# Prompt attention: the value matmuls of a pair of heads alternate on the column halves of the array

## The reference, cut to what matters

```python
def block(i):                      # 128 queries, keys 0 .. 128*(i+1)-1 matter
    s = (einsum('bqhn,bkhn->bhqk', qn, k_nope) + einsum('bqhr,bkr->bhqk', qr, k_rope)) * scale
    s = where(key_pos[None, :] <= q_pos[:, None], s, -inf)
    p = softmax(s, axis=-1)
    return einsum('bhqk,bkhv->bqhv', p, v)
out = lax.map(block, arange(T // 128))
```

## Time and profile before

| what | value |
|---|---|
| median of three runs | 2098.39 us |
| the profiled execution | 2094.72 us |
| its span (first to last instruction) | 2092.9 us |
| PE busy | 1940.1 us, 93% of the span |
| DVE busy, ACT busy | 1298.1 us, 507.9 us |
| prompt attention | from about 508 us to 702 us of the span |
| values L877 | 79.6 us busy, 576 records |
| scores L857 | 76.5 us busy, 192 records |
| turns L690 of `Pr` | 47.5 us busy, 288 records |
| copies of turned probabilities, ACT L1304 | 32.9 us busy, 64 |

### The profile page before, as it was taken

How to read it: one execution, slowest core, us unless ns; L and a number is a source line. 1 busy time by engine, 2 the same in 40 slices (tenths; PEclk the granted TensorE clock), 3 DMA queues, 4 the chain that set the end, 5 groups by cost and what they waited for, 6 DMA issues and landing times.

```text
span 2092.9 us, 34720 instructions
## 1 busy us (share of the span) xinstructions
PE 1940.1 (93%) x15054; PEld 1669.1 (80%) x15054; DVE 1298.1 (62%) x1566; ACT 507.9 (24%) x865; POOL 512.5 (24%) x383
## 2 busy tenths in 40 slices
PE   6989989978999799996989779999999999999988
PEld 5978878876576544446988649999999999999987
DVE  5565665585666688874342545787288277385664
ACT  5222221134543255552120323110011000010013
POOL 2211111221000133431224103232332323323321
PEclk8999999998999899996999989999999999999998
DMA  4101202111000489871122412111211211211112
GB/s 142 41 21 52 52 21 52 39 34 40 1 1 1 181 327 351 327 269 41 51 61 61 154 58 61 41 41 39 63 41 36 60 47 31 61 41 51 46 28 92
DMA packets 157268, 165.12 MB, mean 79 GB/s; under 512 B 18486, under 2 KB 143436, under 8 KB 152988
## 3 DMA queue, kind: packets, MB, share of 16 engines
q1 hardware_dynamic: 142538, 82.70, 13.6%
q0 software_dynamic: 7168, 75.50, 9.5%
q10 hardware_dynamic: 7412, 4.71, 0.7%
HBM read 153.95 MB, written 9.03 MB: 78 GB/s over the span
## 4 chain that ended last, share of the span: by engine, by line
PE 73%; DVE 19%; ACT 4%; issue 2%; DMA 1%; SPq 0%; ACTq 0%; POOL 0%; DVEq 0%
PE PS L671 16%; PE PS L672 15%; PE PS L673 15%; PE PS L690 4%; PE PS L924 4%; PE PS L877 4%; DVE cu L1992 3%; PE PS L954 3%; PE PS L857 3%; PE PS L734 2%; DVE ct L1978 2%; PE PS L914 1%; PE PS L939 1%; DVE Sst L1609 1%; DVE atail L1982 1%
## 5 line engine op out<-in xcount | busy, mean ns | idle before, releaser
L621 POOL CAST whi<-wraw 128x1024 fp32r<-128x1024 f32 (+4 forms) x146 | 131.1, 898 | 1189.7 <-PE PS L673 1064.9
L671 PE MATMUL PS<-BH,whi 128*128 128x344 f32 x1152 | 370.3, 321 | 3.5 <-ACT RB L1136 3.5
L672 PE MATMUL PS<-BL,whi 128*128 128x344 f32 x1152 | 369.2, 320 | 0.0
L673 PE MATMUL PS<-BH,wlo 128*128 128x344 f32 x1152 | 368.9, 320 | 0.0
L623 POOL TENSOR_TENSOR wlo<-wraw,whi 128x1024 fp32r<-128x1024 f32 (+4 forms) x146 | 292.9, 2006 | 11.7
L671 PEld LDWEIGHTS PS<-BH,whi 128*128 128x128 f32 x1152 | 218.1, 189 | 4.0 <-ACT RB L1136 4.0
L672 PEld LDWEIGHTS PS<-BL,whi 128*128 128x128 f32 x1152 | 218.0, 189 | 0.0
L673 PEld LDWEIGHTS PS<-BH,wlo 128*128 128x128 f32 x1152 | 218.0, 189 | 0.0
L1900 DVE TENSOR_TENSOR XT<-PS,XT 128x1032 f32<-128x1032 f32 x56 | 69.0, 1232 | 206.5 <-PE PS L673 206.3
L671 PE MATMUL PS<-XH,whi 128*128 128x344 f32 x528 | 182.8, 346 | 9.6 <-DVE XL L1511 6.1
L672 PE MATMUL PS<-XL,whi 128*128 128x344 f32 x528 | 171.8, 325 | 0.0
(11 more groups left out here) (395 smaller groups left out, 3672.4 us busy)
## 6 DMA issues: line engine op xcount, KB each, us to landing
wraw<-in_w_up_dram SPq DMA_DIRECT2D x44, 512.0 KB, 3.9
wraw<-in_w_in_dram SPq DMA_DIRECT2D x21, 512.0 KB, 4.1
wraw<-in_w_down_dram SPq DMA_DIRECT2D x24, 256.0 KB, 2.9
wraw<-in_w_down_dram SPq DMA_DIRECT2D x16, 320.0 KB, 3.2
xstage<-in_x_prompt_dram SPq DMA_DIRECT2D x8, 512.0 KB, 6.2
wraw<-in_w_out_dram SPq DMA_DIRECT2D x8, 512.0 KB, 4.4
sV<-in_cache_mem_v_dram SPq DMA_DIRECT2D x8, 512.0 KB, 4.7
sK<-in_cache_mem_k_dram SPq DMA_DIRECT2D x8, 512.0 KB, 3.8
```

Of the source, the lines that this page charges most:

```text
L621: gp.tensor_copy(hi, raw).then_inc(w_hi_done, 1)
L671: pe.matmul(out, wh[:, t, 0:m], hi[:, tile(t), s], start=(t == first), stop=False)
L672: pe.matmul(out, wh[:, t, 0:m], lo[:, tile(t), s], start=False, stop=False)
L673: ins = pe.matmul(out, wl[:, t, 0:m], hi[:, tile(t), s], start=False, stop=(t == last))
```

## The change

The values of a pair are no longer computed head by head. PE leaves out the values after an even unit. After the odd unit of the pair it computes both heads: for each key block first the even head's matmul, with its output in partitions 0 to 63, then the odd head's, in partitions 64 to 127. So PE's order within a pair is: turn of the even unit, scores two units on, turn of the odd unit, scores two units on, values of both. The number of matmuls, their shapes and operands, the buffers and the loops of ACT and DVE stay. The semaphore `even_done` goes; ACT and DVE, before they overwrite `PTr[n % 2]`, wait for the values of the whole pair instead.

```diff
-            if u[1] % 2 == 0:
-                use_o = [6 + u[1] // 2 % 2]
-            else:
-                use(("po", u[0], u[1] // 2), use_o, "s")
+            if u[1] % 2:
+                use(("po", u[0], u[1] // 2), [6 + u[1] // 2 % 2], "s")
...
-                if h % 2 == 0:
-                    begin(key)
+                begin(key)
                 for m in range(q + 1):
-                    if m % 4 == 0:
-                        emptied(pe, ("pt", u, m // 4))
-                    r = 64 * (h % 2)
-                    ins = pe.matmul(PS[r:r + 64, uses[key][1][0], 0:P], V[:, m, h * VD:h * VD + VD], PTr[n % 2][:, m, :],
-                                    start=(m == 0), stop=(m == q), skip_group_check=True)
-                if h % 2:
-                    end(ins)
-                else:
-                    ins.then_inc(even_done, 1)
+                    for hh in range(2):
+                        if m % 4 == 0:
+                            emptied(pe, ("pt", units[n + hh - 1], m // 4))
+                        r, c = 64 * hh, (h - 1 + hh) * VD
+                        ins = pe.matmul(PS[r:r + 64, uses[key][1][0], 0:P], V[:, m, c:c + VD], PTr[hh][:, m, :],
+                                        start=(m == 0), stop=(m == q), skip_group_check=True)
+                end(ins)
...
                 if n + 2 < len(units):
                     attention_scores(units[n + 2])
-                attention_values(n, u)
+                if u[1] % 2:
+                    attention_values(n, u)
...
-                    full(act, ("po", units[n - 2][0], units[n - 2][1] // 2)) if units[n - 2][1] % 2 else act.wait_ge(even_done, (n - 2) // 2 + 1)
+                    full(act, ("po", units[n - 2][0], units[n - 2][1] // 2))
...
-                        full(ve, ("po", units[n - 2][0], units[n - 2][1] // 2)) if units[n - 2][1] % 2 else ve.wait_ge(even_done, (n - 2) // 2 + 1)
+                        full(ve, ("po", units[n - 2][0], units[n - 2][1] // 2))
```

More of the change, by code:

```diff
@@ L234, in build_program @@
         trigq_new, q_new, krk_new = sem("trigq_new"), sem("q_new"), sem("krk_new")
-        even_done = sem("even_done")
         p_max, p_new = sem("p_max"), sem("p_new")
```

## The result

The changed kernel takes 2082.76 us (median of four runs, 2080.8 to 2085.62), and the kernel before, run beside it, 2098.51 us: 15.7 us less, a ratio of 0.9923 with a 95% interval of 0.99 to 0.9946. Two later comparisons, each with the kernel before on the same chip, give 14.4 us (0.9928, 0.9907 to 0.9949) and 12.1 us (0.9948, 0.9935 to 0.9961).

What follows compares the result with a forecast made beforehand. It took PE to bound the late pairs, a DVE and ACT loop the early ones, and a new three-engine chain afterwards. Pairs -12.0 and clock +2.5 gave -9.5 us: 2098.4 to 2088.9, range 2084.5 to 2097.

Steps and rivals of the forecast that it cites:

- Two column halves run side by side, 0.0545 us a record: Values' matmuls on PE: records writing different column groups stream side by side, 0.0545 us each; bounds 0.0273 and 0.109.
- The new chain through DVE and ACT: Prompt attention: values wait for the odd head's copy behind DVE and ACT; 8.13 us a pair at q = 7.
- The 0.8 us of idle PE: Sign at the values' load: PE idle for ACT's copy of the odd head, some 0.8 us a pair at q = 7.
- The sum over q = 3 to 7, 12.0 us: Prompt attention: gains of 1.14, 0.83, 0.54, 0.25 and 0.23 us a pair, four pairs each, 12.0 us off.
- The clock, +2.5 us: Pairs at q = 1 and 2: granted clock back after one or two pairs of q = 2; bounds -0.5 and beyond +16.
- The lower end of the range, 2084.5: Whole kernel: 2084.5 us if the new wait is half as long as reckoned and the clock as before.
- The profiled execution as the base: Whole kernel: the profiled execution, 2094.7 us, would take 2085.2; the median of runs is 3.7 above it.
- The rival in which the halves take turns: Values: records of the two halves 0.109 us apart, 9.82 us a pair at q = 7, 12.8 slower, 2111; chance 7%.
- The rival in which the loop is the bound: Prompt attention: pairs fall to DVE and ACT's loop, 7.40 us at q = 7; 2081; 5% with PE as bound.
- PE's need: PE at q = 7: work for a pair falls from 9.27 to about 7.5 us with the values' time halved.

Runs made afterwards that it cites:

- a1_again: The changed kernel again, no edit, with more rounds; 2083.08 us against 2097.52 for the kernel before.
- a4_same_half: Changed kernel with both heads' outputs in one column half and two half-height output copies; 2106.96 us against 2097.52 for the kernel before.
- a3_copy_first: Changed kernel with ACT copying the odd head ahead of the next even unit's exponential, q of 4 and more; 2078.9 us, 0.9898 of the kernel before.

## Why the prediction was wrong, step by step

- *Two column halves run side by side, 0.0545 us a record*: right (30 records in 1.96 us; 3.49 in one half). The rule of the Trainium skill that was weighed (TensorE: Matmul & The Clock Gate, The mechanism), by which loads of the same row group don't run beside matmuls, is not borne out by this either: the 30 loads of that block take 0.137 us each, 4.1 us together, and lie within its 1.96 us.
- *The new chain through DVE and ACT*: right in place and size. Five pair times were within 0.05 us of the forecast (whose terms, as written, add up to 7.99, not 8.01). The 0.8 us of idle PE that it named as a sign shows as 0.28, for the reason given with the timeline.
- *The sum over q = 3 to 7, 12.0 us*: right. In the profile with the clock up to the end (a1_again) these pairs took 12.3 less, of which the last pair 1.18, forecast as 1.14.
- *The clock, +2.5 us*: this is the step that failed, in its size and its sign. I let the clock come back one to two pairs into q = 2, since PE has less to do in q = 1. It came back after the same 23.9 us at 1.2 GHz (three profiles of the changed kernel), inside q = 1, and no pair of q = 2 was slow. And the three pairs that the low clock touches did not lose: from one output copy to the next they take 3.87, 3.78, 4.00 us in the changed profile against 4.01, 4.61 and 4.41 before, 1.4 us less. Part of this is chance, for the clock fell at 508.3 us in that profile of before and at 506.0 in the changed one. Over the four profiles of before the three pairs add up to 13.03, 12.32, 12.99 and 12.09 us, over the three of the changed kernel to 11.66, 11.75 and 11.96: 0.8 us less on average. The term was about -0.8 where the forecast had +2.5, and that is 3.3 of the 6.1 us by which it was off. The lower end of the range, 2084.5, took the clock "as before", at 0.
- *What is left*: with -0.8 the sum is -12.8 and the forecast 2085.6, inside the range; the measured gain was 15.7. The stages are 11.6 to 13.8 us shorter, one profile against another. The three comparisons gave 15.7, 14.4 and 12.1 us, and the interval of each holds 12.8. The sample attention varies by 7 us from one profile to another on like chips. I take the last 2.9 us for that spread, which makes it luck that the first comparison came out at the far end; this is argued and not shown. No run shows a gain outside the stage, and none excludes one of 1 us.
- *The profiled execution as the base*: it ran 2094.7 us and the changed one 2085.6, only 9.1 apart, though the stage was 12.3 shorter. The stage began 0.6 us later in the changed one, and what follows it took 2.5 us longer, with a sample attention of 230.7 us against 225.2. That the profile of before was a short one could not be seen from one execution.
- *The rival in which the halves take turns*: its pair times were good (9.82 forecast, 9.61 measured in a4_same_half; the extra of 1.69 us in it measured as 1.53), but I took it for the whole of what the change did. Most of the gain doesn't need alternation: head by head at the new place already gives 9.9 us. I had not seen that the even head's block runs under the wait for the odd head's copy.
- *The rival in which the loop is the bound*: it was the next bound, not this one; a3_copy_first shows it at 7.38 us in three of four pairs at q = 7.

## What to carry to other kernels

When a reordering frees the busiest engine, follow the dependencies through the other engines for one period before crediting the saving: here PE's need fell to 7.5 us, by the prediction's estimate, and the period to 8.08. Then ask what already runs inside the new wait: making that faster (here the even head's block) is worth only what sticks out of it, and moving the awaited copy ahead of the exponential on ACT was worth 4.2 and 5.9 us more. For terms that rest on the state of the clock, give a range on both sides of zero rather than a signed correction, and take a second profile of before where a later stage has a spread of its own.

## What the hardware showed that I had not expected

- Two blocks that write different column halves overlap at their seam without any interleaving: 32 records in 3.33 us, where 0.109 us each would make 3.70. By the spacing of the starts the odd head's first record starts with the even head's thirteenth of sixteen. In one half no two records start together (30 in 3.49 us).
- A change between 64 and 128 stationary columns costs PE about 0.13 us (8.76 against 9.27 us a pair, for four of them, at q = 7).
- The granted clock came back after 23.9 us in both kernels though PE was given less to do (busy 20.7 us of them against 20.9), and fell at 686.9 us in one execution and at 693.9 in another of the same kernel, which was worth 1.4 us.
- The same program took 26 us more on one chip; the sample attention, which gathers pages, took 257 us there against 225 to 230.
